# Hybrid attention and MoE layer on one core: gate matrix as split chunks, y rows in slot order, one block loop, embedding kept on chip

## What is computed

```python
    f = rms_norm(h, g_ffn)                      # (512, 1024)
    logits = f @ w_router + b_router            # 32 experts
    top_vals, top_idx = top_k(logits, 4); gates = softmax(top_vals)
    # rows sorted by expert; every row block is multiplied by its own expert's weights
    hid = xb @ w1[e] + b1[e]                    # 1024 -> 2048
    y = clamped_swiglu(hid) @ w2[e] + b2[e]     # 1024 -> 1024
    h = h + sum over a token's 4 experts of gate * y
    ple = rms_norm(p @ w_ple_proj, g_ple)
    h = h + sigmoid(h @ w_ple_gate) * ple
    return rms_norm(h, g_final)
```

## Time and profile before

| | us |
|---|---|
| median of 3 runs | 1656.46 (1654.59 to 1658.42) |
| the profiled execution | 1657.01 |
| its span | 1655.2 |
| PE busy | 1570.3 (95%) |
| DVE busy | 1267.8 (77%) |
| ACT busy | 985.6 (60%) |
| POOL busy | 126.9 (8%) |
| chain that ended last: PE's share | 92% |
| of it w1 products (L1077), w2 products (L1102), gate products (L1171) | 43%, 22%, 3% |

### The profile page before, as it was taken

The page is one execution under the profiler, slowest core; times in us unless marked ns, Lnnn a source line. Parts: engine busy times, 40 slices in busy tenths (PEclk is TensorE's granted clock), DMA queues, the critical chain, the costliest instruction groups (busy, mean ns, idle before and its releaser), DMA issues.

```text
span 1655.2 us, 19957 instructions
## 1 busy us (share of the span) xinstructions
PE 1570.3 (95%) x6909; PEld 1063.3 (64%) x6909; DVE 1267.8 (77%) x1038; ACT 985.6 (60%) x881; POOL 126.9 (8%) x114
## 2 busy tenths in 40 slices
PE   5999899975999999999999999999999999999987
PEld 3887555552666666666666666666666666666533
DVE  4413233336699999999999999999999999999663
ACT  5422222222677777777777777777777777777411
...
GB/s 158 52 101 291 125 13 6 8 167 137 288 388 373 373 377 385 376 368 370 372 379 376 384 368 366 366 385 379 380 372 368 371 373 386 378 375 370 233 279 51
DMA packets 132689, 482.83 MB, mean 292 GB/s; under 512 B 9235, under 2 KB 9782, under 8 KB 132662
## 3 DMA queue, kind: packets, MB, share of 16 engines
...
## 4 chain that ended last, share of the span: by engine, by line
PE 92%; DVE 2%; issue 2%; ACT 1%; DMA 1%; POOL 0%; ACTq 0%; SPq 0%; POOLq 0%; DVEq 0%
PE ps L1077 43%; PE ps L1102 22%; PE ps L908 8%; PE ps L923 4%; PE ps L1171 3%; PE ps L1086 2%; PE ps L968 1%; PE ps L1065 1%; PE ps L1109 1%; PE ps L1045 1%; PE ps L990 1%; DMA XG<-f_rows,tokix 1%; PE ps L1149 1%; PE ps L942 1%; PE ps L980 1%
## 5 line engine op out<-in xcount | busy, mean ns | idle before, releaser
L1418 DVE TENSOR_TENSOR HL<-W,HL 128x2048 fp32r<-128x2048 f32 x384 | 872.8, 2287 | 68.2 <-ACT HL L710 62.3
L710 ACT ACTIVATE HL<-W 128x2048 fp32r<-128x2048 f32 x384 | 734.7, 1915 | 208.0 <-PE ps L1077 115.2
L1077 PE MATMUL ps<-HL,XTh 128*96 128x512 f32 x2048 | 562.5, 396 | 3.4 <-DVE XTl L1414 2.0
L1077 PEld LDWEIGHTS ps<-HL,XTh 128*96 128x96 f32 x2048 | 323.9, 162 | 134.5 <-DVE HL L1418 2.3
L1077 PE MATMUL ps<-HL,XTl 128*96 128x512 f32 x1024 | 320.1, 393 | 0.0
L1102 PE MATMUL ps<-HL,HIDTh 128*96 128x512 f32 x1024 | 282.3, 397 | 2.5 <-issue 2.5
L1102 PEld LDWEIGHTS ps<-HL,HIDTh 128*96 128x96 f32 x1024 | 160.2, 161 | 80.3 <-issue 17.5
L1077 PEld LDWEIGHTS ps<-HL,XTl 128*96 128x96 f32 x1024 | 164.9, 161 | 70.8
L1102 PE MATMUL ps<-HL,HIDTl 128*96 128x512 f32 x512 | 159.4, 392 | 0.0
L547 POOL DMA_INDIRECT XG<-f_rows,tokix x33 | 64.4, 1953 | 1032.2 <-PE ps L1065 1031.9
L1102 PEld LDWEIGHTS ps<-HL,HIDTl 128*96 128x96 f32 x512 | 82.2, 160 | 35.1
...
## 6 DMA issues: line engine op xcount, KB each, us to landing
W<-in_w_dram SPq DMA_DIRECT2D x384, 1024.0 KB, 8.5
...
wst<-in_w_out_dram SPq DMA_DIRECT2D x2, 2048.0 KB, 16.7
...
```

The lines of the kernel that those rows point to most:

```text
L710: act.activation(HL[:, k % HRING, 0], w_slot(k), ACT.Copy).then_inc(w_hi, 1)
L1077: last = pe.matmul(ps[0:CAP, 2 * h + n], xt[:, c], HL[:, s, part, cc * 1024 + n * 512:cc * 1024 + (n + 1) * 512], start=(c == 0 and xt is ...
L1418: dve.tensor_tensor(HL[:, k % HRING, 1], w_slot(k), HL[:, k % HRING, 0].bitcast(F32), ALU.subtract).then_inc(w_lo, 1)
```

## The change

Five things:

- **Gate's matrix as chunks.** `w_ple_gate` is loaded as four more 1 MB chunks into W slots 0 to 3 (`load_gate`), ahead of the last two w2 chunks on SP, split by ACT (`gate_hi`) and DVE (`gate_lo`) into HL, and multiplied in three fp32r products instead of one of fp32. ACT and DVE split h too (`h2Th`, `h2Tl`).
- **y rows in slot order.** DVE sorts each token's four slots (and gates, `gate2`) by slot number. The first three of a token then lie in blocks before the last, so POOL gathers these three for tile 0 once the last block but one is stored. The gathers land in other places (`yg(s)`), some of which wait for gate splits.
- **One loop for all blocks.** Every engine runs one loop over `n + 31` blocks. SP reads both experts of a block from `tab`, which now has an entry for every block. The bias choice goes by block number: `pair` has a column for each block.
- **Normed embedding on chip.** No `ple_rows`. Tiles were moved so that `pleo` stays. g_ple is loaded after block 0's chunks, and POOL multiplies by it after gather 1. g_final is loaded when PE has used the last chunk.
- **First gather moved up.** POOL's gather 0 stands before the last embedding tile's two operations.

Beside these: the last tile of the tail goes in two halves, ACT copies two of the b2 results out of PSUM, and one more block of y rows is zeroed at the start. The core of the diff:

```diff
...
+        actf = actT[:].rearrange("p c n -> p (c n)")
+        gple = actf[:, 0:D]
+
+        def yg(s):
+
+            if s < 3:
+                return actf[:, s * D:(s + 1) * D]
+            if s < 7:
+                return w_slot(4 + (s - 3) // 2)[:, (s - 3) % 2 * D:((s - 3) % 2 + 1) * D]
+            if s < 15:
+                return W[:, (s - 7) * D:(s - 6) * D]
+            return actf[:, 3 * D:4 * D]
...
-                    body(i)
-            return n
+        def load_gate(sp, b, g):
+            sp.dma_start(w_slot(g).rearrange("p (c n) -> p c n", c=2),
+                         w_ple_gate[0, 256 * g:256 * (g + 1), :].rearrange("(c p) n -> p c n", p=P)).then_inc(w_in_s[g], 16)
+
+        def tail_parts(t):
+            return [(0, D)] if t < NT - 1 else [(0, 512), (512, D)]
+
+        def extra_count(eng):
+            return eng.value_load(tab[0:1, NBLK:NBLK + 1], min_val=0, max_val=NEXTRA)
 
         block = ctx.enter_context(nc.Block())
 
...
                 load_chunk(sp, 0, k, 0)
-            for t in range(NT):
-                sp.wait_ge(pp_out, t + 1)
-                sp.dma_start(ple_rows[t * P:(t + 1) * P, :], pleo[:, t]).then_inc(ple_stored, 16)
             for k in range(6, 10):
                 sp.wait_ge(w_lo, k - 5)
                 load_chunk(sp, 0, k, 0)
-            sp.wait_ge(ple_stored, 16 * NT)
+            sp.wait_ge(pp_done, NT)
             for k in range(10, NK):
                 load_chunk(sp, 0, k, 0)
-            with sp.Fori(1, NE) as b:
-                load_expert(sp, b, b, b - 1)
+            sp.wait_ge(bb_ready, BB_PARTS)
+            sp.dma_start(gple, g_ple[0].partition_broadcast(P)).then_inc(gple_in, 16)
             sp.wait_ge(tab_ready, 1)
-
-            def body(i):
-                before_e = sp.value_load(tab[0:1, bass.ds(i, 1)], min_val=0, max_val=NE - 1)
-                e = sp.value_load(tab[0:1, bass.ds(i + 1, 1)], min_val=0, max_val=NE - 1)
-                load_expert(sp, i + NE, e, before_e)
-            n = extra_blocks(sp, body)
-            last_e = sp.value_load(tab[0:1, bass.ds(n, 1)], min_val=0, max_val=NE - 1)
+            n = extra_count(sp)
+            with sp.Fori(0, n + (NE - 1)) as i:
+                b = i + 1
+                before_e = sp.value_load(tab[0:1, bass.ds(b - 1, 1)], min_val=0, max_val=NE - 1)
+                e = sp.value_load(tab[0:1, bass.ds(b, 1)], min_val=0, max_val=NE - 1)
+                load_expert(sp, b, e, before_e)
+            last_e = sp.value_load(tab[0:1, bass.ds(n + (NE - 1), 1)], min_val=0, max_val=NE - 1)
+            for g in range(4):
+                sp.wait_ge(w_lo, (n + NE) * NK + (g - 7))
+                load_gate(sp, n + NE, g)
             for k in (4, 5):
                 sp.wait_ge(w_lo, (n + NE) * NK + (k - 7))
                 load_chunk(sp, n + NE, k, last_e)
-            wg_v = w_ple_gate[0].rearrange("(c p) n -> p c n", p=P)
-            for i in range(2):
-                if i == 1:
-                    sp.wait_ge(w_lo, (n + NE) * NK)
-                sp.dma_start(wpg[:, i], wg_v[:, :, i * 512:(i + 1) * 512]).then_inc(wst_in[i], 16)
...
-            for t in range(NT):
+            def gather(b):
+
+                if b > 0:
+                    pool.wait_ge(xt_done, b)
+                pool.indirect_dma_start(XG[:], None, f_rows, bass.IndirectOffsetOnAxis(ap=tokix[:, b:b + 1].bitcast(U32), axis=0)).then_inc(xg_in, 16)
+
+            for t in range(NT):
+                if t == NT - 1:
+                    pool.wait_ge(tab_ready, 1)
+                    pool.wait_ge(f_stored, 16 * NT)
+                    gather(0)
                 pool.wait_ge(pp_ss, t + 1)
                 link(pool.tensor_scalar(ss[:, 5:6], ss[:, 7:8], 1.0 / D, EPS, ALU.mult, ALU.add))
                 pool.tensor_tensor(rstd[:, 5:6], ss[:, 5:6], mhalf[:, 0:1], ALU.pow).then_inc(pp_rs, 1)
                 pool.wait_ge(pp_rs, t + 1)
 
...
+            for b in range(1, NE + 1):
                 gather(b)
-            n = pool.value_load(tab[0:1, NEXTRA + 1:NEXTRA + 2], min_val=0, max_val=NEXTRA)
+                if b == 1:
+                    pool.wait_ge(gple_in, 16)
+                    pool.wait_ge(pp_out, NT)
+                    for t in range(NT):
+                        pool.tensor_tensor(pleo[:, t], pleo[:, t], gple, ALU.mult).then_inc(ple_scaled, 1)
+            n = extra_count(pool)
...
+            def gather_y(s):
+                pool.indirect_dma_start(yg(s), None, y_rows, bass.IndirectOffsetOnAxis(ap=sloti[:, s:s + 1].bitcast(U32), axis=0)).then_inc(yg_in[s], 16)
+
+
+
+            pool.wait_ge(slots_sorted, 1)
             pool.wait_ge(ple_scaled, NT)
+            def stored(blocks, k):
+                pool.wait_ge(y_stored, blocks * 16)
+                pool.tensor_tensor(held[:], tok[0:1, 0:1], tok[0:1, 0:1], ALU.add).then_inc(blocks_done, 1)
+                pool.wait_ge(blocks_done, k)
+
+            stored(n + (NE - 1), 1)
+            for s in range(3):
+                gather_y(s)
+            stored(n + NE, 2)
+            gather_y(3)
+            for s in range(4, NT * TOPK):
+                if s == 4:
+                    pool.wait_ge(gate_split, 1)
+                if 9 <= s < 15 and s % 2 == 1:
+                    pool.wait_ge(gate_split, (s - 7) // 2 + 1)
+                gather_y(s)
+
...
+                expert_block(b, True)
+            act.wait_ge(tab_ready, 1)
+            n = extra_count(act)
+            with act.Fori(0, n + (NE - 2)) as i:
+                expert_block(i + 2)
             sigmoid(n + (NE - 1), 1)
             split_hi(n + NE, 4, 0)
             move_out(n + (NE - 1), 1)
             split_hi(n + NE, 5, 0)
+
+            def gate_hi(g):
+                act.wait_ge(w_in_s[g], landed(n + NE, g))
+                act.wait_ge(piece_used, (n + NE) * NK + (g - 3))
+                act.activation(HL[:, (2 + g) % HRING, 0], w_slot(g), ACT.Copy).then_inc(w_hi, 1)
+
+            for g in range(3):
+                gate_hi(g)
             store_y(n + (NE - 1), (n + NE) * NK)
-            act.wait_ge(y_stored, (n + NE) * 16)
-            act.activation(held[:], tok[0:1, 0:1], ACT.Copy).then_inc(blocks_done, 1)
+            gate_hi(3)
+            for t in (2, 3):
+                act.wait_ge(b2_done, t + 1)
+                act.activation(OUTB[:, 3 - t], ps[:, B2_BANK[t]:B2_BANK[t] + 2].rearrange("p a n -> p (a n)"), ACT.Copy).then_inc(b2_out, 1)
 
...
                         last = pe.transpose(ps[:, i, c * P:(c + 1) * P], H[:, t, (4 * i + c) * P:(4 * i + c + 1) * P], ident[:])
...
                 if t >= 2:
                     pe.wait_ge(gm_sig, t - 1)
-                for n in range(2):
+                for i in range(2):
                     for c in range(NC):
-                        last = pe.matmul(ps[:, 2 + 2 * (t % 2) + n], actT[:, c, t * P:(t + 1) * P], wpg[:, n, c],
-                                         start=(c == 0), stop=(c == NC - 1))
-                    if n == 0 and t < NT - 1:
+                        g = c // 2
+                        if t == 0 and i == 0 and c % 2 == 0:
+                            pe.wait_ge(gate_split, g + 1)
+                        at = (c % 2) * D + i * 512
+                        for ht, part in ((h2Th, 0), (h2Th, 1), (h2Tl, 0)):
+                            last = pe.matmul(ps[:, 2 + 2 * (t % 2) + i], ht[:, t % 2, c], HL[:, (2 + g) % HRING, part, at:at + 512],
+                                             start=(c == 0 and ht is h2Th and part == 0), stop=(c == NC - 1 and ht is h2Tl))
...
+            place = it_b[:, 0:TOPK].unsqueeze(1).unsqueeze(3).to_broadcast([P, NT, TOPK, TOPK])
+            link(dve.tensor_tensor(cmp4[:], place, ord4[:].rearrange("p (t k) -> p t k", k=TOPK).unsqueeze(2).to_broadcast([P, NT, TOPK, TOPK]), ALU.is_equal))
+            pick = prod[:, 0:8].rearrange("p (h a) e -> p h (a e)", h=4)[:, 0:1, 0:64].rearrange("p o (t r k) -> p (o t) r k", t=NT, r=TOPK)
+            link(dve.tensor_tensor(pick, cmp4[:], gate[:].unsqueeze(2).to_broadcast([P, NT, TOPK, TOPK]), ALU.mult))
+            link(dve.tensor_reduce(gate2[:].rearrange("p (t k) -> p t k", k=TOPK), pick, AX.X, ALU.add))
+            link(dve.tensor_tensor(pick, cmp4[:], by_t.unsqueeze(2).to_broadcast([P, NT, TOPK, TOPK]), ALU.mult))
+            link(dve.tensor_reduce(ord4[:].rearrange("p (t k) -> p t k", k=TOPK), pick, AX.X, ALU.add))
+            dve.tensor_copy(sloti[:], ord4[:]).then_inc(slots_sorted, 1)
...
+            def gate_lo(g):
+                dve.wait_ge(w_hi, (n + NE) * NK + (g + 1))
+                dve.tensor_tensor(HL[:, (2 + g) % HRING, 1], w_slot(g), HL[:, (2 + g) % HRING, 0].bitcast(F32), ALU.subtract).then_inc(gate_split, 1)
...
+            def rest_h2(t):
+                for i in range(2):
+                    dve.wait_ge(h2h_out, 2 * t + i + 1)
+                    dve.tensor_tensor(h2Tl[:, t % 2, 4 * i:4 * i + 4], ps[:, i].rearrange("p (c q) -> p c q", c=4),
```

(28 more changed lines are left out.)

225 lines of the change are left out of this document (107 added, 118 removed).

## The result

| | before | after |
|---|---|---|
| median, same chip (us) | 1658.4 (8 runs, 1654.59 to 1664.31) | 1651.33 (8 runs, 1643.54 to 1652.8) |
| ratio, 95% interval | | 0.9942 (0.9926 to 0.9957) |
| profiled execution, span | 1657.01, 1655.2 | 1652.45, 1650.6 |

The kernel got faster, by 0.58% or 9.6 us. The forecast was 16.7 us and 1640; the direction held, the time lies above the range's upper end of 1650. The forecast had started from the earlier median of 1656.46, though, and the measured ratio takes that to 1646.9, inside the range. So two questions: which terms of the sum came out, and where the missing 7 us are.

A forecast was written before the change was run, and what follows sets the result against it. PE was taken to set the loop's pace, DVE and DMA close behind, so gains had to come from the seams. -8.4 + 5.0 + 0 - 13.3 = -16.7 us gave 1640 us, range 1630 to 1650.

The forecast's parts named there:

- The loop. 0 us: Block loop: SP's added table reads, zeroing one more block of y rows and moved tiles cost nothing, 0 us.
- The head: Before the loop: earlier first gather, DVE late next through slot sorting; PE starts chunk 0 at 407.7, not 416.1, -8.4 us.
- Scaling in block 0: Block 0: POOL's four g_ple operations cost DVE 6.9 to 9.4 us if g_ple lands late; +5 us (0 to 9).
- The end of the loop: Last w2 chunks land later, sharing DMA queues with gate chunks and early y gathers; +1.5 us (0 to 5).
- The start of tile 0: Tail: early adds and gate splits hidden in the store's shadow; PE starts gate products at 1583.4, not 1585.85.
- The gate products and the end: Tail: fp32r products 11.25 us per tile against 13.90, 50.4 in all; halving the last tile saves 2.0 of 10.1 us.
- The rival of a DVE-bound tail: Tail: DVE's 55.8 us of work makes PE wait 2 to 3 us per tile; gain 5 us only, 1648; chance 0.20.
- Scaling for nothing: Block 0 and loop end: g_ple lands early, scaling is free, last chunks aren't late; 1632 us; chance 0.17.
- Table reads: Loop: SP's two reads per block delay its loads and reach PE, 0.74 us a block, 23 us; 1663; chance 0.06.
- for what I don't see: Whole kernel: chance 0.07 left for outcomes that neither the forecast nor any named rival covers.

## Why the prediction was right in direction and 7 us short

**The step that failed is "The loop. 0 us".** It looked at instructions added and at who waits, and dismissed the rest with "the moved tiles are hidden: nobody waits for them". True, and beside the point: a moved tile isn't an operation that can hide, it changes how long every product on it takes. It cost 6.6 us, 0.21 a block on 31 blocks, and the shift in the kernel before reproduces all of it (1105.9 to 1112.5 us for the same stretch). How the place makes a product longer stays open. PE is the engine that sets the loop's pace, so nothing there covers even the 1.5 ns that each of a block's 144 products (96 of w1, 48 of w2) became longer. The table of stretches misses the forecast by 6.4 us in all, and this term alone by 6.6; the others nearly cancel.

**The head: right.** -8.7 for -8.4, with DVE late next as the step had it. Sorting cost 1.5 us against 2.1. The single run of the gather alone shows what the term is worth without it: 10.2 us.

**Scaling in block 0: right in mechanism, in size partly by luck, +6.3 for +5.** The load landed at 426, behind the 415 to 423 of the step, and DVE lost 7.3 us, within the stated 6.9 to 9.4. The run without the operations takes all of it back (27.9 us). But "PE pays nearly all of it" did not hold: PE's pauses grew by 4.4 us, and the other 2.7 are the clock that fell behind them, which the step didn't have. The Trainium skill ("SBUF — State Buffer", Who interferes with whom) has the two engines take turns for a whole instruction; the trace agrees in both directions: L1496 ran 2.89 us instead of 0.69, longer by about one POOL operation's 2.34 at its shortest, and one of POOL's four, started at 437.2 beside back-to-back splits, took 12.1 us, as the row of all four shows (ns min/median/max):

```profile
L569 POOL TENSOR_TENSOR wst<-wst,actT x4: 2803/4202/12105, 426.1 to 437.2; 128x1024 f32<-128x1024 f32 x4
```

**The end of the loop: right in size, wrong in cause.** ACT did wait 2.30 us for a chunk of w2, but PE's pause before the last 24 products is 2.56 us, as before. What made the stretch 1.7 us longer is the clock right behind that pause. The stretches 1571 to 1574 of the changed kernel and 1559 to 1562 of the one before (PE, PEld, DVE, ACT, POOL, granted clock):

```profile
1571.00:1574.00 3.00, 3.00 (x8) 1.94 (x7) 3.00 (x2) 3.00 (x2) 0.00 (x0) 0.50 0.00 0
```
```profile
1559.00:1562.00 3.00, 2.28 (x10) 1.61 (x10) 2.29 (x1) 0.52 (x1) 0.00 (x0) 1.00 0.33 119
```

In both PE had paused some 2.5 us and then worked; once the clock fell to 0.50, the lower of its two levels (1.2 of 2.4 GHz), once it didn't. In the four profiles of the kernel before and its variants it never fell there (pauses of 2.5 to 2.7 us, the stretch 14.7 to 14.9); in the ten of the changed kernel and its variants it fell in seven (pauses of 2.0 to 3.4 us, the stretch 15.7 to 17.8), and not in the three others (1.5 to 2.4 us, then a second pause; 14.5 to 15.4). So the term is real on the average, by way of the clock. Why the clock falls in one family and not in the other after equal pauses wasn't settled.

**The start of tile 0: mis-sized by 1.7 us.** 14.8 us from b2's products against 16.5. The 1.5 us for POOL beside DVE's splits didn't fall on the path: the gather that counts is the first of its group and took 0.95 us as always; ones behind it took up to 2.00.

**The gate products and the end: right.** 50.6 for 50.4 and 8.3 for 8.1; a fp32r product took 0.23 us at the upper clock level. PE's only wait between tiles is 1.28 us. The rival of a DVE-bound tail would have cost 2 to 3 us per tile, and falls. Its time of 1648 is the nearest of all to the median, for the wrong reason.

**The rivals.** Scaling for nothing: falls (6.3 us). Table reads: fall, the loop without them is the same. A case of its own for tiles that get another address was missing; it would have been the 7% "for what I don't see". The median of the kernel before was 1658.4 in the runs that decide and 1656.46 in those shown first, another 2 us of the distance between 1640 and 1651.
